# Moving a strip preparation, a column sum and a residual scaling in a two-block transformer kernel

## What is computed

```python
x = rmsnorm(h, final_norm_g)            # end of the first block
# second block
h2 = rms_norm(x, mix_pre_g)
proj = h2 @ w_in                        # dt, GLU, state-space strips, gates
...
mixed = (g_conv * conv_out + g_ssm * ssm_out) @ w_out
x = x + rms_norm(mixed, mix_post_g)     # residual: needs x itself
h2 = rms_norm(x, ffn_pre_g)
...
x = x + rms_norm(f, ffn_post_g)
```

## Time and profile before

| what | value |
|---|---|
| median of 3 runs | 2170.16 us (2169.98 to 2170.24) |
| the profiled execution | 2169.9 us |
| its span in the trace | 2168.0 us |
| mean granted TensorE clock | 0.957 |
| PE busy | 2003.7 us (92%) |
| DVE busy | 1007.4 us (46%) |
| ACT busy | 1123.8 us (52%) |
| POOL busy | 272.1 us (13%) |

### The profile page before, as it was taken

One profiled execution on the slowest core, in us unless ns is written; L12 is line 12 of the kernel. 1 busy time (PEld: TensorE's weight loads), 2 busy tenths in 40 slices (PEclk: granted clock), 3 DMA queues, 4 the chain that ended last, 5 costly groups with the idle time before them and its releaser, 6 DMA issues.

```text
span 2168.0 us, 26573 instructions
## 1 busy us (share of the span) xinstructions
PE 2003.7 (92%) x9386; PEld 1621.2 (75%) x9386; DVE 1007.4 (46%) x1634; ACT 1123.8 (52%) x1530; POOL 272.1 (13%) x318
## 2 busy tenths in 40 slices
PE   5888789889899999999999999998999989999996
PEld 4677656568578888887877787887877868888885
DVE  4246643223434223144788776667752334223134
ACT  6535544344444333344547888767846454334342
POOL 1100000001011111110111110110111101111110
PEclk9999878789999999998999999999999989999998
DMA  9834435348358888885877676785777867888884
GB/s 251 182 78 98 96 79 117 88 106 186 88 129 191 187 191 192 186 193 127 205 175 165 151 171 156 196 203 136 181 181 188 187 136 177 192 190 191 190 181 100
DMA packets 95624, 347.83 MB, mean 160 GB/s; under 512 B 10624, under 2 KB 10624, under 8 KB 94880
## 3 DMA queue, kind: packets, MB, share of 16 engines
q0 software_dynamic: 45216, 163.60, 41.6%
q1 hardware_dynamic: 46656, 170.19, 27.2%
q10 hardware_dynamic: 3648, 12.65, 1.7%
HBM read 342.14 MB, written 4.26 MB: 160 GB/s over the span
## 4 chain that ended last, share of the span: by engine, by line
PE 72%; DVE 11%; ACT 8%; DMA 4%; issue 3%; DVEq 2%; ACTq 1%; SPq 0%
PE bank L339 21%; PE bank L340 20%; PE bank L341 20%; DVE ssum L1636 4%; DMA arena<-scratch 2%; ACT wl L774 2%; ACT wh L773 2%; DMA wl<-in_weights 1%; PE work L401 1%; PE work L492 1%; PE work L442 1%; ACT arena L1047 1%; DVE xt L1673 1%; PE work L480 1%; PE work L549 1%
## 5 line engine op out<-in xcount | busy, mean ns | idle before, releaser
L773 ACT ACTIVATE wh<-raw 128x1024 fp32r<-128x1024 f32 x314 | 332.2, 1058 | 788.1 <-PE bank L341 731.8
L339 PE MATMUL bank<-XAh,wh 128*128 128x512 f32 (+1 forms) x1712 | 671.9, 392 | 31.2 <-DMA wl<-in_weights 25.6
L340 PE MATMUL bank<-XAl,wh 128*128 128x512 f32 (+1 forms) x1712 | 659.8, 385 | 0.0
L341 PE MATMUL bank<-XAh,wl 128*128 128x512 f32 (+1 forms) x1712 | 659.1, 385 | 0.0
L755 POOL DMA_DIRECT2D wl<-in_weights x314 | 271.9, 866 | 1860.8 <-ACT wl L774 1823.3
L339 PEld LDWEIGHTS bank<-XAh,wh 128*128 128x128 f32 x1712 | 328.7, 192 | 102.0 <-DMA wl<-in_weights 26.5
L341 PEld LDWEIGHTS bank<-XAh,wl 128*128 128x128 f32 x1712 | 327.7, 191 | 63.8
L340 PEld LDWEIGHTS bank<-XAl,wh 128*128 128x128 f32 x1712 | 328.8, 192 | 60.8 <-issue 0.7
L774 ACT ACTIVATE wl<-raw 128x1024 fp32r<-128x1024 f32 x314 | 327.4, 1043 | 0.0
L339 PE MATMUL bank<-XBh,wh 128*128 128x512 f32 x752 | 298.5, 397 | 3.2 <-DMA wl<-in_weights 3.2
L341 PE MATMUL bank<-XBh,wl 128*128 128x512 f32 x752 | 297.0, 395 | 0.0
(11 more groups left out here) (301 smaller groups left out, 1819.7 us busy)
## 6 DMA issues: line engine op xcount, KB each, us to landing
raw<-in_weights SPq DMA_DIRECT2D x306, 512.0 KB, 6.9
wl<-in_weights POOLq DMA_DIRECT2D x306, 512.0 KB, 8.0
arena<-scratch ACTq DMA_DIRECT2D x16, 512.0 KB, 7.9
raw<-in_weights SPq DMA_DIRECT2D x8, 384.0 KB, 3.6
wl<-in_weights POOLq DMA_DIRECT2D x8, 384.0 KB, 5.7
h<-in_xT SPq DMA_DIRECT2D x2, 1024.0 KB, 6.7
spill<-cst ACTq DMA_DIRECT2D x8, 256.0 KB, 7.2
arena<-spill ACTq DMA_DIRECT2D x1, 2048.0 KB, 11.4
```

The lines of the kernel that those rows point to most:

```text
L339: mm(bank[s][:, 0:w], hi, tile(X[0], k, w), start=(n == 0), stop=False)
L340: mm(bank[s][:, 0:w], hi, tile(X[1], k, w), start=False, stop=False)
L341: last = mm(bank[s][:, 0:w], lo, tile(X[0], k, w), start=False, stop=(n == len(kts) - 1))
L773: act_(wh[j % 4][:, :], raw[j % 2][:, :], ACT.Copy)
```

## The change

Three things are changed.

1. At the end of the first block and in `w_out2`, ACT squares the last tile first, takes the root of the column sums, and only then does the `step` of the last strip.
2. `norm_cols` sends the column sums of `ssum` ahead of the wait for the last square, and sums the bank as one accumulation group.
3. The residual is not scaled in the GLU loop. The spread of `pre` moves on PE from behind the first strip pair to behind the first strip of `w_out2`, into work bank 1; DVE's copy to `rstd` goes, and its eight scalings move into the `w_out2` loop, reading the work bank.

```diff
                 w = work_bank(("norm", k), 3)
                 pe.wait_ge(ssum_rdy, k + 1)
-                if done is not None:
-                    pe.wait_ge(sq_done, done)
-                for c in range(TT):
-                    last = mm(w[:, c:c + 1], (total or ssum)[:, c * P:(c + 1) * P], ones[:, 0:1], start=True,
-                              stop=done is None)
-                    if done is not None:
-                        last = mm(w[:, c:c + 1], sq[:, 1, c * P:(c + 1) * P], ones[:, 0:1], start=False, stop=True)
+                parts = [(total or ssum)] + ([] if done is None else [sq[:, 1, :]])
+                for n, part in enumerate(parts):
+                    if n:
+                        pe.wait_ge(sq_done, done)
+                    for c in range(TT):
+                        last = mm(w[:, c:c + 1], part[:, c * P:(c + 1) * P], ones[:, 0:1], start=(n + c == 0),
+                                  stop=(n == len(parts) - 1 and c == TT - 1))
                 last.then_inc(wk_done[3], 1)
...
             strip_pair(AT["dt"], XA, tiles_from("pre"))
-            norm_spread(NORM["pre"], 2)
...
                 strip(AT["w_out2"] + n, XA, xn=tiles_from("mix") if n == 0 else None)
+                if n == 0:
+                    norm_spread(NORM["pre"], 2, 1)
...
-                step(AT["ffn1"] + 48 + u)
+                if u < 15:
+                    step(AT["ffn1"] + 48 + u)
...
             root_cols(NORM["final"], EPS * EPS)
+            step(AT["ffn1"] + 63)
...
-                step(j)
+                if n < KT - 1:
+                    step(j)
...
             root_cols(NORM["post"])
+            step(AT["w_out2"] + KT - 1)
...
-            r = wait_full(dve, ("spread", NORM["pre"]))
-            free(copy(rstd[:, :], r[:, :]), ("spread", NORM["pre"]))
-            dve.drain()
...
-                STT(tile(h, t), tile(h, t), V("final_g", t), rstd[:, :], ALU.mult, ALU.mult)
...
+            def scale_residual(n):
+
+                r = wait_full(dve, ("spread", NORM["pre"]))
+                ins = STT(tile(h, n), tile(h, n), V("final_g", n), r[:, :], ALU.mult, ALU.mult)
+                if n == KT - 1:
+                    free(ins, ("spread", NORM["pre"]))
+
             for n in range(KT):
                 dve.drain().then_inc(h_upd, 1)
                 if n:
                     sum_square(n - 1, SQN["post"] + n - 1)
+                    scale_residual(n - 1)
             dve.drain().then_inc(ssum_rdy, 1)
+            scale_residual(KT - 1)
             cols_recip(NORM["post"])
```

More of the change, by code:

```diff
@@ L379, in norm_cols, with norm_spread @@
                 pe.wait_ge(ssum_rdy, k + 1)
-                if done is not None:
-                    pe.wait_ge(sq_done, done)
-                for c in range(TT):
-                    last = mm(w[:, c:c + 1], (total or ssum)[:, c * P:(c + 1) * P], ones[:, 0:1], start=True,
-                              stop=done is None)
-                    if done is not None:
-                        last = mm(w[:, c:c + 1], sq[:, 1, c * P:(c + 1) * P], ones[:, 0:1], start=False, stop=True)
+                parts = [(total or ssum)] + ([] if done is None else [sq[:, 1, :]])
[5 more added lines that the diff above has]
+                                  stop=(n == len(parts) - 1 and c == TT - 1))
                 last.then_inc(wk_done[3], 1)
-            def norm_spread(k, n):
-                w = work_bank(("spread", k), 2)
+            def norm_spread(k, n, b=2):
+                w = work_bank(("spread", k), b)
                 pe.wait_ge(sem("n_rr"), n)
@@ L394, in norm_spread @@
                     last = mm(w[:, c * P:(c + 1) * P], s_nr[:, c:c + 1].broadcast_to([P, P]), ident, start=True, stop=True)
-                last.then_inc(wk_done[2], 1)
+                last.then_inc(wk_done[b], 1)
             def turn_tile(key, b, src, n=TT):
```

## The result

| kernel | median | range | ratio to before, 95% interval |
|---|---|---|---|
| before | 2170.07 us (6 runs) | 2165.83 to 2175.36 | |
| changed | 2153.60 us (6 runs) | 2151.13 to 2159.97 | 0.9928 [0.9912, 0.9944] |

The changed kernel is 15.6 us faster by the ratio, between 12.2 and 19.1; 16.5 by the medians. That is 0.7% of the time, and clear of the noise. The forecast was 13.6. The two profiled executions differ by 16.6 us (spans 2168.0 and 2151.4).

The account below looks back on a forecast made before the run. PE bounds most of the span, DVE the GLU loop to about 1160 us. Gains of 1.1, 2.0 (final), 6.3 (GLU), 1.9, 1.25, 1.0 (post), 0.9 (ffpost), less 0.8, made 13.6: 2156.6 us, range 2153.0 to 2163.5.

Parts of the forecast that it names:

- Square first: In `final` and `post`, ACT's last square starts sooner, ahead of the strip passes: gains of 1.09 and 1.91 us.
- The moved step at nothing: In `final` and `post`, the step behind the root costs nothing; 1.3 us left over in `final` before the next ACT work.
- Column sums: Four `ssum` pairs run while PE waits for the square: gains 2.03 us in `final`, 1.25 `post`, 0.9 `ffpost`.
- Rival B: In the three norms, PE's queue holds early sums until the square, so they give nothing: 2159.3 us, chance 0.06.
- The clock of the spreads: Earlier spread runs at full clock in `post`, gaining 1.0 us; 0 counted in `final` and `ffpost`.
- Rival C: PE's clock stays up through the spreads of `final`, `post` and `ffpost`: 2154.6 us, chance 0.10.
- DVE in the GLU loop: Eight scalings leave DVE, which leads there, so PE resumes 6.3 us earlier.
- Rival A: The GLU gain doesn't reach the end, as a weight or broadcast behind 1160 us arrives last: 2162.9 us, chance 0.22.
- Spread in `w_out2`: Four spread matmuls behind the first strip of `w_out2`, where PE leads, add 0.8 us, between 0.4 and 2.05.
- Rival D: Shifted weight stream makes the 15 broadcasts each land 1.9 us later, 28.5 us in all: 2185.1 us, chance 0.06.

Follow-up runs that it names:

- e10: The changed kernel, untouched, run and profiled once more: 2156.50 us, ratio 0.9936 to the kernel before.
- e1: Kernel before with only the squares first and the step behind the root, in `final` and `post`: 2167.44 us, ratio 0.9972.
- e4: Changed kernel with the last strip's step between square and root, in `final` and `post`: 2161.37 us, ratio 0.9936.
- e2: Kernel before with only the `ssum` column sums moved ahead of the wait for the last square: 2171.05 us, ratio 0.9982.
- e3: Kernel before with only the residual's scaling and its spread moved to `w_out2`: 2170.45 us, ratio 0.9982.
- e9: Changed kernel with two depthwise convolution parts moved from GLU loop to group 6, and redundant wide matmuls in PE's waits of `final`: 2145.06 us, ratio 0.9879.
- e5: Changed kernel with eight scalings added to DVE's GLU loop, written to an unused tile: 2158.46 us, ratio 0.9947.
- e6: Changed kernel with one depthwise convolution part (four taps) moved from tile 4 of the GLU loop to group 6: 2154.66 us, ratio 0.9945.
- e7: Changed kernel with two depthwise convolution parts (eight taps) moved from the GLU loop to group 6: 2150.99 us, ratio 0.9916.
- e8: Changed kernel with redundant 128x512 matmuls before and behind the spreads of `final` and `post`: 2155.09 us, ratio 0.9931.

## Why the prediction was right

The forecast of 2156.6 us is 3.0 us above the median, and its 13.6 us are inside what the ratio allows (12.2 to 19.1); the second set of runs of the same kernel, e10, gives 13.9. The median of 2153.60 us is 0.6 us above the lower end of the range of 2153.0 to 2163.5, and 0.4 us under the narrower one of the forecast itself (2154 to 2159.5); e10's 2156.50 is inside both. By its own steps:

- **Square first.** 1.09 us in `final` and 1.91 in `post` were priced; the square starts 0.07 us behind the add, and `post` gave 1.91. Shown by e1.
- **The moved step at nothing.** 1.3 us were to be left over in `final`; it is 1.37. The strips that the moved step prepares didn't wait for weights. That it must stand behind the root, e4 showed: +1.17 and +1.42 us otherwise.
- **Column sums.** 2.03, 1.25 and 0.9 us were priced. `final` as a whole is 3.19 us shorter, forecast 3.12; `post` gave 1.26; `ffpost` 1.03. Rival B (the queue holds them) falls with e2. That the sizes fit so well has luck in it: `post` was priced from one execution, where the eight pairs took 3.00 us up to the root, and in e3 the same instructions took 4.00, so that the same step would have been worth 2.26.
- **The clock of the spreads.** 0, 1.0 and 0 us were priced, measured 0.02, 0.93 and 0. The 0.93 is the upper end of what comes: over the ten profiles that have the square first, the root of `post` stands 4.12 to 4.63 us before the first high tile, and 5.05 without, so the gain is 0.4 to 0.9. Rival C was that the clock stays up in all three places. The Trainium skill (TensorE: Matmul & The Clock Gate, What's actually happening) says the engine's clock follows how busy it has been recently. Rival C took the early sums to be enough for that, and they weren't: in `final` and `ffpost` the spreads took 2.02 and 2.05 us. That redundant matmuls in the waits ahead of the sums and of the spread do keep it up, 1.13 us in e9, agrees with the Trainium skill. The rival's 2154.6 us is nearer to the median than the forecast is; it's the traces that decide against it, not the time.
- **DVE in the GLU loop.** 6.3 us were priced, measured 6.22. The operations themselves are 5.8 to 6.1 of it; the rest is the gaps, 1.27 us before and 0.88 after, which weren't in the forecast and happened to move its way. That the SiLU comes 6.2 us sooner is shown by e3, and by e5 that it's the eight operations. Rival A (a later wait takes them) predicted 2162.9 us and a loss in the groups. Each of the twelve runs of the changed kernel is faster than that (2160.72 us is the slowest), so it falls as a whole. The groups spread by 13 us between executions with no order by edit, so a loss of 1 or 2 us there can't be excluded.
- **Spread in `w_out2`.** 0.8 us priced, 0.95 measured: 0.81 for the spread, and 0.14 which first matmuls behind it take longer. DVE was never last.
- **Rival D** (broadcasts come later) would have cost 28 us in the groups. The stretch from the SiLU to `w_out2` took 569.74 and 560.90 us in the two executions of the changed kernel, 568.26 before.

Summed, the touched stretches give 14.1 us against 13.6, and 0.35 of the 14.1 is the gap at the end, which was not forecast. The rest of the 16.6 is the execution's own.

One reading was mistaken without changing the sum. The prediction has DVE lead up to the SiLU, "to about 1160 us", and the expectations of e6 and e7 took PE's 3 us there for the rest of that lead. e7's 6.75 us show the lead to reach on into group 0.

## What to carry to other kernels

When the runs of one kernel spread by 10 us, compare stretches between instructions that are tied by semaphores. Here those at one clock repeat to a few hundredths of a microsecond (109.14 to 109.18 us from the first GLU product to the SiLU in the five profiles that share that code), and a gain of 1 us is plain in one trace that whole runs can't show. Where the clock falls within a stretch, the same instructions differ by up to 1 us, and one trace isn't enough. A stretch led by an engine that is busy 47% over the span is worth every instruction that leaves it; and PE's visible wait there gives no upper bound for the gain (6.75 us in e7, with a wait of 3.2), since the next waits shrink too. In a chain of small steps (square, sums, root, spread), put everything that is not in the chain behind the last step that has a successor waiting.

## What the runs showed of the hardware that was not expected

- In the changed kernel's `final`, sums and spread ran with waits of only 0.80 and 0.69 us between them, and still the granted clock fell to its lower level, 1.2 GHz: the spread took 2.02 us. With redundant 128x512 matmuls in these waits (e9) it took 1.13, at 2.4 GHz, as in `post` of the changed kernel. With them only around the spread (e8) it took 1.83.
- The same eight pairs of column sums took 3.00, 4.00 and 2.70 us from the square to the root of `post` (before, e3, e1), by where the clock fell among them. With four pairs left behind the square it was 1.72 to 1.75 us there in all nine profiles that have the early sums, but e4's, where the step stood ahead. In `ffpost` the four pairs don't always escape: 1.77 us in six profiles and 1.88 to 2.13 in four.
- DVE shows gaps of 0.43 to 0.66 us that wait for nothing, at places that differ between programs and stay the same between executions of one. They also come and go with edits elsewhere in the loop: e5, with eight operations added to the changed kernel's loop, has none of them in the loop. What makes them was not tried.
